# Query and key turns with the tokens stationary, and softmax weights turned by transfers and VectorE

## The reference, cut to what matters

```python
qkv = (x @ w_qkv).reshape(bsz, seqlen, 3, ATTN_HEADS, ATTN_HEAD_DIM)
q, k, v = qkv[:, :, 0], qkv[:, :, 1], qkv[:, :, 2]
...
q = (_partial_rope(q, cos, sin) * (ATTN_HEAD_DIM ** -0.5)).transpose(0, 2, 1, 3)
k = _partial_rope(k, cos, sin).transpose(0, 2, 1, 3)
...
s_own = jnp.where(k_pos[None, :] <= q_pos[:, None], s_own, NEG_INF)
...
p = jax.nn.softmax(s, axis=-1).astype(v.dtype)
...
o = o.transpose(1, 0, 3, 2, 4).reshape(bsz, seqlen, ATTN_HEADS * ATTN_HEAD_DIM)
return o @ w_out
```

## Time and profile before

| | us |
|---|---|
| median of 3 runs | 2096.89 (2096.42 to 2096.99) |
| profiled execution, its own time | 2096.86 |
| its span, first to last instruction | 2095.0 |
| TensorE (PE) busy | 2085.9 |
| VectorE (DVE) busy | 1290.4 |
| ScalarE (ACT) busy | 975.1 |

### The profile page before, as it was taken

One profiled execution on the slowest core, in us unless ns is written; L12 is line 12 of the kernel. 1 busy time (PEld: TensorE's weight loads), 2 busy tenths in 40 slices (PEclk: granted clock), 3 DMA queues, 4 the chain that ended last, 5 costly groups with the idle time before them and its releaser, 6 DMA issues.

```text
span 2095.0 us, 28820 instructions
## 1 busy us (share of the span) xinstructions
PE 2085.9 (100%) x9918; PEld 1749.5 (84%) x9918; DVE 1290.4 (62%) x1246; ACT 975.1 (47%) x1172; POOL 21.3 (1%) x16
## 2 busy tenths in 40 slices
PE   9999999999999999999999999999999999999999
PEld 8898888888888888888988888888888888888887
DVE  6869666665555565555766667675665554555565
ACT  5596455434444443443644445454434443443442
POOL 0000010000000000000000000010000000000000
PEclk9999999999999999999999999999999999999999
DMA  7665758766766766775654556658666766766763
GB/s 257 195 197 189 235 180 261 250 200 203 236 222 183 238 230 201 219 233 171 193 186 158 168 167 225 202 189 267 216 210 212 241 206 195 243 218 228 241 212 120
DMA packets 233547, 439.80 MB, mean 210 GB/s; under 512 B 15056, under 2 KB 37840, under 8 KB 232432
## 3 DMA queue, kind: packets, MB, share of 16 engines
q1 hardware_dynamic: 232032, 432.79, 65.2%
q10 hardware_dynamic: 1424, 5.77, 0.7%
HBM read 419.63 MB, written 18.87 MB: 209 GB/s over the span
## 4 chain that ended last, share of the span: by engine, by line
PE 99%; DMA 0%; ACT 0%; issue 0%; DVE 0%; ACTq 0%
PE ps L427 75%; PE ps L419 11%; PE ps L416 5%; PE ps L726 1%; PE ps L725 1%; PE ps L724 1%; PE ps L558 1%; PE ps L739 0%; DMA wst<-in_rg_w_in_dram 0%; PE ps L524 0%; PE ps L523 0%; PE ps L525 0%; PE ps L596 0%; PE ps L714 0%; PE ps L599 0%; PE ps L575 0%
## 5 line engine op out<-in xcount | busy, mean ns | idle before, releaser
L1014 DVE TENSOR_TENSOR wl<-wst,wh 128x1024 fp32r<-128x1024 f32 x743 | 887.8, 1219 | 327.3 <-ACT wh L757 324.0
L757 ACT ACTIVATE wh<-wst 128x1024 fp32r<-128x1024 f32 x743 | 769.8, 1059 | 649.1 <-PE ps L427 411.8
L427 PE MATMUL ps<-wh,hid 128*128 128x512 f32 x2560 | 695.9, 390 | 0.0
L427 PEld LDWEIGHTS ps<-wh,hid 128*128 128x128 f32 x2560 | 479.5, 188 | 98.9
L427 PE MATMUL ps<-wh,xin 128*128 128x512 f32 x2048 | 548.9, 389 | 0.0
L427 PEld LDWEIGHTS ps<-wh,xin 128*128 128x128 f32 x2048 | 383.9, 188 | 79.4
L427 PE MATMUL ps<-wl,hid 128*128 128x512 f32 x1280 | 404.6, 389 | 0.0
L419 PE MATMUL ps<-xin,wh 128*128 128x512 f32 x960 | 331.2, 395 | 0.8 <-DVE wl L1014 0.8
L427 PE MATMUL ps<-wl,xin 128*128 128x512 f32 x1024 | 315.2, 389 | 0.0
L427 PEld LDWEIGHTS ps<-wl,hid 128*128 128x128 f32 x1280 | 240.2, 188 | 50.0
L416 PE MATMUL ps<-xin,wl 128*128 128x256 f32 x960 | 256.8, 278 | 0.0
(11 more groups left out here) (138 smaller groups left out, 835.9 us busy)
## 6 DMA issues: line engine op xcount, KB each, us to landing
wst<-in_mlp_w_dram SPq DMA_DIRECT2D x512, 512.0 KB, 4.7
wst<-in_moba_w_qkv_dram SPq DMA_DIRECT2D x96, 512.0 KB, 4.6
wst<-in_rg_w_in_dram SPq DMA_DIRECT2D x62, 512.0 KB, 4.1
wst<-in_rg_w_out_dram SPq DMA_DIRECT2D x32, 512.0 KB, 4.9
sq_by_quad<-f SPq DMA_DIRECT2D x128, 128.0 KB, 2.5
f<-sq_by_quad SPq DMA_DIRECT2D x32, 512.0 KB, 5.1
wst<-in_moba_w_out_dram SPq DMA_DIRECT2D x32, 512.0 KB, 5.3
f<-in_x_dram SPq DMA_DIRECT2D x8, 256.0 KB, 6.3
```

The source lines that it names most:

```text
L427: return pe.matmul(banks(half)[:, a, :], src[:, c, part, a * P:(a + 1) * P], (wl if low else wh)[:, s, w], start=(c == 0 and part + low == 0),
L757: act.activation(wh[:, off % SPLITS, :], wst[:, slot, :], ACT.Copy).then_inc(wh_done, 1)
L1014: dve.tensor_tensor(wl[:, off % SPLITS, :], wst[:, off % STAGE, :], wh[:, off % SPLITS, :], ALU.subtract).then_inc(wl_done, 1)
```

## The change

Five things are changed together.

1. Query and key turns become `token_turn()`, and the value turn uses the same function. The first query turn becomes `begun_token_turn()`. The stage's turns use the PSUM banks 0 to 3, the scores 4 to 7, the weighted sums 6 and 7.
2. Queries and keys come out with tokens on partitions. ScalarE writes them by 32-column parts (`take_qk`), 16 transfers within SBUF (32 partitions by 1 KB each; SyncE issues eight, ScalarE eight) move the parts, and VectorE transposes squares of 32 x 32 (`rotate`) before the rotation. There is no `take_hl` and no addition.
3. The softmax weights are scaled into such parts by three multiplications (`softmax_end`), moved by 16 transfers (32 partitions by 1.5 KB) and transposed by VectorE (`turn_p`). TensorE's transposes and ScalarE's four copies are gone.
4. The scores are made before the last block of the value turn instead of before the fifth. Exponentials, scaling, moving and the weighted sums come in the next group's query turn and after the first block of its key turn. Those of the last group come in the output product: the sums before its ninth block. The output product's first two turns are run in an interleaved order (`held_pair`), with the last group's inputs late.
5. Keys are rotated on VectorE ahead of all splits of the value turn.

The core of the diff:

```diff
@@ SyncE
-            with sp.Fori(0, NG) as g:
-                for part in range(3):
-                    load_turn(moba_w_qkv[0], part * D + g * COLS,
-                              B_QKV + (3 * g + part) * BLOCKS)
+            def move_qk(g, part):
+                sp.wait_ge(qk_evict, HALVES * (2 * g + part + 1))
+                if 2 * g + part:
+                    sp.wait_ge(qk_ready, 2 * g + part)
+                for dst, src in part_moves(qk_quad, qk_out, (0, 1)):
+                    sp.dma_start(dst, src).then_inc(qk_moved, 16)
+
+            def move_p(g):
+                sp.wait_ge(p_ready, g + 1)
+                for dst, src in part_moves(prob_quad, prob_out, (0, 1)):
+                    sp.dma_start(dst, src).then_inc(p_moved, 16)
+
+            for g in range(NG):
+                k_before = {2: lambda: move_qk(g - 1, 1)} if g else {}
+                p_before = {BLOCKS - 2: lambda: move_p(g - 1)} if g else {}
+                for part, also in enumerate((k_before, p_before, {2: lambda: move_qk(g, 0)})):
+                    load_turn(moba_w_qkv[0], part * D + g * COLS, B_QKV + (3 * g + part) * BLOCKS, also)
@@ TensorE
+            for g in range(NG):
+                b = B_QKV + 3 * g * BLOCKS
+                own, other = 2 * (g % 2), 2 * (1 - g % 2)
+                if g == 0:
+                    begun_token_turn(1, b, R_LN1)
+                else:
+                    pe.wait_ge(qk_evict, HALVES * 2 * g)
+                    token_turn(xin, own, b, R_LN1)
+                    pe.wait_ge(v_stored, g)
+                token_turn(xin, other, b + BLOCKS, R_LN1, {1: lambda: weighted(g - 1)} if g else {})
+                pe.wait_ge(qk_evict, HALVES * (2 * g + 1))
+                token_turn(xin, own, b + 2 * BLOCKS, R_LN1, {BLOCKS - 1: lambda: scores(g)})
@@ ScalarE
+            for g in range(NG):
+                b, no = B_QKV + 3 * g * BLOCKS, B_QKV // BLOCKS + 3 * g
+                own, other = 2 * (g % 2), 2 * (1 - g % 2)
+                if g:
+                    exponentials(g - 1)
+                splits(b, no, START, START + 1)
+                if g:
+                    move_p(g - 1)
+                splits(b, no, START + 1, LATE + 1)
+                take_qk(g, 0, own)
+                splits(b, no, LATE + 1, NEXT)
+                b, no = b + BLOCKS, no + 1
+                splits(b, no, START, START + 1)
+                if g:
+                    weighted_hi(g - 1)
+                splits(b, no, START + 1, LATE + 1)
+                take_qk(g, 1, other)
+                splits(b, no, LATE + 1, NEXT)
+                b, no = b + BLOCKS, no + 1
+                splits(b, no, START, LATE + 1)
+                act.wait_ge(mm_done, b + BLOCKS)
+                act.activation(vg, ps[:, own:own + 2, :], ACT.Copy).then_inc(v_stored, 1)
+                splits(b, no, LATE + 1, NEXT)
@@ VectorE
+            def turn_p(g):
+                dve.wait_ge(p_moved, MOVES * (g + 1))
+                dve.transpose(f2[:, 1536:3072].rearrange("p (b i t) -> p i b t", i=GROUP, t=32),
+                              prob_quad.rearrange("p i (b r) -> p i b r", r=32)).then_inc(pt_ready, 1)
...
+            for g in range(NG):
+                b = B_QKV + 3 * g * BLOCKS
+                if g:
+                    splits(b, START, START + 1)
+                    softmax_end(g - 1)
+                    splits(b, START + 1, LATE)
+                    turn_p(g - 1)
+                    splits(b, LATE, NEXT)
+                else:
+                    splits(b, START, NEXT)
+                b += BLOCKS
+                splits(b, START, START + 2)
+                if g:
+                    weighted_lo(g - 1)
+                rotate(g, 0, qg)
+                splits(b, START + 2, START + 3)
+                rotated(g, 0, qg)
+                splits(b, START + 3, NEXT)
+                b += BLOCKS
+                rotate(g, 1, kg)
+                rotated(g, 1, kg)
+                splits(b, START, LATE + 1)
+
+                dve.wait_ge(scores_done, g + 1)
```

## The result

The changed kernel takes 2107.7 us (median of 5, 2104.24 to 2108.97), beside 2096.79 for the kernel before (median of 5). The ratio is 1.0047, 95% interval 1.0036 to 1.0059: slower by about 10.9 us, where 2086.6 was forecast, and outside the range.

The account below looks back on a forecast made before the run. TensorE, busy 2085.9 of 2095.0 us, was taken as the bound. From 2096.86 us, 11.4 saved and 1.1 of last-group wait returned gave 2086.6 us; range 2085.0 to 2092.7, chance 0.83.

Parts of the forecast that it names:

- The saving: TensorE's attention stage: 3.40 + 0.97 us from query and key turns, 7.00 from softmax transposes, together 11.4 us.
- the turns' part: Query and key turns in token form: 3.40 us saved, plus 0.97 on the begun first query turn.
- Rival (c): TensorE's stream goes by columns alone, so only the transposes' saving is left: 2091.0 us; chance 0.04.
- TensorE asks at 21.76 + 2.72 = 24.5: on time by 1.6 us: Weighted sums, first three groups: softmax transpose done 22.9 us after the value turn's end, before TensorE needs it.
- late by 1.1 us: Last group's weighted sums: TensorE asks at 21.76 us, after eight output-product blocks, and waits 1.1 us for the transpose.
- An issue at 0.46 us: Each small transfer's issue on ScalarE: median of similar transfers with a short gap, 3.7 us for eight.
- The keys' part: From the key turn's end: VectorE's transpose starts at 8.3 us, keys ready at 14.6, covered by 4.4 us.
- at 2.1 us: Mask addition on VectorE, behind the sixth value-turn split ending at 24.0 us: 2.1 us late.
- Rival (a): Softmax chain late in every group; waits eat the saving at 3.8 us delay, near 0.70 us per issue; chance 0.12, half slower.
- x: Delay in us to VectorE's softmax transpose beyond the forecast; TensorE's waits sum to 3(x - 1.6) + (x + 1.1).
- Rival (b): Moves land in 5.1 us, not 2.5: 2087.9 us; strong end, with 0.6 us per issue, 2092, up to 2092.7, chance 0.11.
- Rival (d): SyncE's waits starve the weight splits once 16 us of cover are gone: 2100 us and more; chance 0.05.

Follow-up runs that it names:

- c1_pool_later: Changed kernel with GpSimd issuing ScalarE's moves and the weighted sums asked for three blocks later; 2085.27 us, ratio 0.9943 to the kernel before.
- e7_qk_alone: Changed kernel with the softmax half undone: TensorE transposes the weights, ScalarE copies them out; query and key turns stay changed; 2091.06 us, ratio 0.9972.
- e6: Changed kernel with one value-turn split on VectorE before the keys' transpose and one before their last addition; 2096.79 us, ratio 1.0000.
- e4_kfirst: Changed kernel with SyncE's key moves two weight loads earlier, in the last group also ahead of the LayerNorm rows; 2122.37 us, ratio 1.0115.
- e3_sp_only: Changed kernel with all 16 transfers of every move issued by SyncE, none by ScalarE; 2144.85 us, ratio 1.0222.
- e5b: Changed kernel with unread filler matmuls on TensorE before the weighted sums, 6 in the first group and 13 in the last; 2106.07 us, ratio 1.0042.
- e2: Changed kernel with ScalarE's eight issues per move given to GpSimd; 2091.9 us, ratio 0.9968.
- a_again: Changed kernel unaltered, run again against the kernel before; 2107.09 us, ratio 1.0048.

## Why the prediction was wrong

**The saving was right.** 11.4 us were forecast; c1_pool_later, which does all of TensorE's new work with no wait in the stage, is 11.9 below its kernel before. In its trace the stage, counted as in the sum above, takes 305.7 us (1002.12 to 1316.00, less the three blocks by which the sums are later), and 317.35 - 11.4 is 306.0. e7_qk_alone keeps the turns' part, 4.4 us, and covers the four waits of 0.28 us for ScalarE's copy, 1.1 us: that is a ratio of 0.9974, and 0.9972 was measured. Rival (c), that the turns save nothing, is thereby excluded.

**The step that failed is "TensorE asks at 21.76 + 2.72 = 24.5: on time by 1.6 us", and for the last group "late by 1.1 us".** The measured waits there are 3.3, 0.9, 1.9 and 8.6 us. The mechanism, the chain and its order were as described; the terms were too small, and they added up on a margin of 1.6 us:

- An issue at 0.46 us. ScalarE's softmax issues have a median of 0.61, and eight take 5.5 us, not 3.7. That is 1.8 us in each group, more than the margin by itself. e6's last group shows it nearly alone: bias at 3.3, forecast 3.4, transpose at 24.8 instead of 22.9, and a wait of 3.0 instead of 1.1.
- The keys' part "transpose from 8.3, ready at 14.6". The transpose started 3.2 us late in group 0 and 5.4 in the last. ScalarE is done with the copies and issues at 6.7 instead of 5.0, so 1.7 of each is its own. VectorE's two splits ahead of the transpose then end at 10.3 and 11.8 instead of 8.3; in the last group ScalarE stood 1.6 us for weights between them. And then VectorE waits another 1.3 and 2.0 us for the transfers. In group 0 SyncE's half, put at the same time as ScalarE's, stands behind a weight load and ends at 9.5. In the last group SyncE is done at 6.9, but the transfers take 6.3 to 7.6 us to land instead of 2.5.
- What follows from late keys was in the prediction, but at 2.1 us: the value turn's splits start late, the buffers come free late, and the mask addition stands behind the sixth split. It was 5.6 and, in the last group, 8.4 us late.

**Rival (a) is what happened**: the measured waits of 14.6 us are those of x = 4.6 in its formula, beyond its 3.8. But x was not one number: it was 5.0, 2.6, 3.6 and 7.6 in the four groups. The rival got 0.12, half of it for slower. Its threshold was 0.70 us for an issue; with the gaps, eight in 5.5 us are 0.69 each and the keys' eight in 5.0 are 0.63. By its own pricing that makes x = 1.8 + 0.8 = 2.6 and waits of 6.7 us, so by this estimate the issues on ScalarE account for about half, and the rest came from late loads, SyncE's place in its own order and the last landing. Rival (b)'s long landing occurred in the last group's key move only, and longer than its 5.1. Its strong end was also added up wrongly: x near 3 gives, by the formula in (a), 4 x 3 - 3.7 = 8.3 us of waits and about 2093.8, not 2092; the range's upper end of 2092.7 rested on it. Rival (d) was wrong as put: TensorE never waited for a weight block. But its mechanism worked in another way, by the splits that stand ahead of the keys and of the mask addition, which have no 16 us of cover; e4_kfirst and e3_sp_only show that price at 14 and 38 us.

**Not priced at all** was TensorE's clock behind a wait. It is near 5.3 of the 21.8 us lost, but e5b shows that holding it gives nothing that can be measured, as long as the chain behind is late.

**What stays open.** Whether the LayerNorm rows or the weight loads ahead of them made the last key transfers land late is not separated. Nor is the gain of e6_reorder split between the earlier buffer and the shorter wait at low clock. Why groups 1 and 2 are less late than group 0 is not explained here.

## What to carry to other kernels

When work leaves the bounding engine for a chain of copies, issues, landings and another engine's queue, give the consumer a due time with several us of slack, not the place where the arithmetic just fits: moving the sums by three blocks and one split ahead of the keys turned 10 us lost into 10 us gained. Count every DMA issue at the rate of its own shape on its own queue, and count on each engine what stands before the new instruction, above all the loads that a late split holds back. A short wait removed by filler is not time gained while the next result is late.

## What the runs showed of the hardware

- Issuing a transfer of 32 partitions within SBUF takes 0.59 us in the median on SyncE's queue and 0.61 on ScalarE's, up to 1.31, and 0.50 in the median on GpSimd's (e2). The squares' transfers to DRAM take 0.43. For these small moves issuing is the larger part: eight take 5.0 to 5.5 us, and a transfer lands 2.0 to 2.6 us behind its issue in the median. The Trainium skill ("DMA: Bandwidth & Descriptors", Issuing engines are not separate DMA queues) calls the initiation time that several issuing engines save "usually small relative to the DMA itself"; here the measurement decides otherwise, by 38 us between e3_sp_only and the changed kernel.
- The same small transfers land 1.8 to 2.2 us after their issue when they go out ahead of 2 MB of rows and two weight blocks (e4, DMA share 0.38 from 1280.7 to 1287.5), and 6.3 to 7.6 behind them (changed kernel, DMA share 1.0).
- TensorE's clock is at its 1.2 GHz level right after waits of 2.62 (a_again), 2.97 (e6), 3.27, 4.46 (e2) and 8.63 us, and at 2.4 GHz right after 0.86, 1.86, 2.02 (a_again) and 2.31 (e6); in e5b_filled it fell 1.4 us into the products behind a wait of 2.95. It does not come back after a fixed time: in the changed kernel all 5.15 us of products and part of the next matmuls run at the low level (the first four take 1.35 and 1.56 us, 1.17 at full clock; the next four 1.07 and 1.09), while in e2, after 4.46 us of waiting, it is back within 2.7 us (the third pair of products takes 0.74 us, the fourth 0.60).
